# The expert chain of a decoder trunk set one pair further behind its gathers, its last phase written out

## The reference, cut to what matters

```python
s = jnp.einsum('nhie,ike->nhik', q, keys)          # 8 heads x 2 x 128 key scores per token
top_s, top_i = lax.top_k(s, 16)
...                                                # 16x16 candidates, the best 16 of them
idx  = jnp.take_along_axis(cand_i, best_pos, axis=-1)
gate = jax.nn.softmax(best_s, axis=-1)
u    = expert_u[idx]                               # 128 experts per token, each a row of 1024
act  = jax.nn.gelu(jnp.einsum('nhkd,nd->nhk', u, xb), approximate=False)
coef = gate * act
out  = jnp.einsum('nhk,nhkd->nd', coef, expert_v[idx])
h = h + out
```

## Time and profile before

| | before |
|---|---|
| median of three executions | 1802.99 us |
| the profiled execution: span | 1814.9 us |
| TensorE busy | 1521.3 us (84%) |
| VectorE busy | 1176.7 us (65%) |
| POOL busy | 597.8 us (33%) |
| ScalarE busy | 526.2 us (29%) |
| moved by DMA | 666.65 MB, mean 367 GB/s |

### The profile page before, as it was taken

The page is one execution under the profiler, slowest core; times in us unless marked ns, Lnnn a source line. Parts: engine busy times, 40 slices in busy tenths (PEclk is TensorE's granted clock), DMA queues, the critical chain, the costliest instruction groups (busy, mean ns, idle before and its releaser), DMA issues.

```text
span 1814.9 us, 18537 instructions
## 1 busy us (share of the span) xinstructions
PE 1521.3 (84%) x5336; PEld 826.6 (46%) x5336; DVE 1176.7 (65%) x3357; ACT 526.2 (29%) x1139; POOL 597.8 (33%) x588
## 2 busy tenths in 40 slices
PE   6858799897867899898988669989989888877776
PEld 3535343443544577454445436765544444432222
DVE  2478756655878666666458885666763778955554
ACT  0123212421233244353113323534521223321111
POOL 1032243443322322222332223333232334455442
PEclk9979799998988899999999889999989989999999
DMA  8399799999988799999998779999989989999997
GB/s 341 140 363 356 289 392 424 416 421 405 413 343 343 294 373 422 353 362 354 391 420 335 310 303 337 402 419 382 360 298 424 404 347 393 386 409 421 422 422 303
DMA packets 84050, 666.65 MB, mean 367 GB/s; under 512 B 9376, under 2 KB 9520, under 8 KB 10880
## 3 DMA queue, kind: packets, MB, share of 16 engines
q0 software_dynamic: 74464, 540.13, 74.9%
q1 hardware_dynamic: 9216, 124.47, 16.6%
q10 hardware_dynamic: 288, 1.05, 0.1%
HBM read 664.55 MB, written 1.05 MB: 367 GB/s over the span
## 4 chain that ended last, share of the span: by engine, by line
PE 52%; DVE 24%; DMA 12%; issue 5%; ACT 5%; POOL 1%; ACTq 0%; POOLq 0%; DVEq 0%; SPq 0%; PEldq 0%
PE acc L732 30%; DMA ring<-in_experts,idx_now 11%; PE act_bank L483 9%; DVE ring L1272 7%; PE dve_bank L469 6%; PE act_bank L669 3%; DVE scratch L939 3%; ACT diag L902 2%; DVE scratch L1182 1%; DVE scratch L1183 1%; DVE scratch L1185 1%; DVE scratch L1181 1%; ACT scratch L773 1%; DVE scratch L1184 1%; PE dve_bank L649 1%
## 5 line engine op out<-in xcount | busy, mean ns | idle before, releaser
L732 PE MATMUL acc<-ring,diag 128*128 128x512 f32 x2048 | 1007.5, 630 | 258.3 <-ACT diag L902 251.1
L411 POOL DMA_INDIRECT ring<-in_experts,idx_now x512 | 570.9, 1115 | 910.2 <-PE acc L732 815.5
L1272 DVE CUSTOM_DVE_ANT_0 ring<-ring,hn 128x1024 f32<-128x1024 f32 x512 | 623.4, 1224 | 252.3 <-DMA ring<-in_experts,idx_now 235.9
L732 PEld LDWEIGHTS acc<-ring,diag 128*128 128x128 f32 x2048 | 383.1, 198 | 724.9 <-issue 423.7
L895 ACT ACTIVATE acts<-dots 128x2 f32<-128x2 f32 x256 | 52.1, 204 | 766.8 <-DVE dots L1272 760.8
L483 PEld LDWEIGHTS act_bank<-hnT,wbuf 128*128 128x128 f32 x1920 | 245.8, 202 | 55.1 <-issue 55.1
L902 ACT ACTIVATE diag<-cst,coefs 128x128 f32<-128x128 f32 x512 | 177.9, 394 | 248.9 <-DVE coefs L1280 224.9
L483 PE MATMUL act_bank<-hnT,wbuf 128*128 128x128 f32 x1920 | 245.8, 284 | 1.2 <-ACT hnT L773 1.2
L773 ACT ACT_TABLE_LOAD x82 | 105.2, 1283 | 23.2 <-PE act_bank L669 14.4
L406 POOL COPY idx_now<-idx 128x8 uint32 x64 | 21.4, 334 | 260.8 <-PE acc L732 186.6
L1280 DVE TENSOR_TENSOR coefs<-acts,gate 128x2 f32<-128x2 f32 x256 | 41.2, 161 | 92.4 <-ACT acts L895 81.5
(11 more groups left out here) (112 smaller groups left out, 819.4 us busy)
## 6 DMA issues: line engine op xcount, KB each, us to landing
wbuf<-in_weights SPq DMA_DIRECT2D x56, 2048.0 KB
ring<-in_experts,idx_now POOLq DMA_INDIRECT x512
kept<-in_weights SPq DMA_DIRECT2D x2, 2048.0 KB, 14.6
gains<-in_gains SPq DMA_DIRECT2D x2, 512.0 KB, 8.5
scratch<-in_bias POOLq DMA_DIRECT2D x1, 1024.0 KB, 7.8
gains<-in_gains ACTq DMA_DIRECT2D x2, 512.0 KB, 10.3
out<-h SPq DMA_DIRECT2D x2, 512.0 KB, 8.8
scratch<-in_bands POOLq DMA_DIRECT2D x1, 768.0 KB, 4.5
```

Of the source, the lines that this page charges most:

```text
L411: pool.indirect_dma_start(ring[:, s], None, io[f"experts{layer}"], bass.IndirectOffsetOnAxis(idx_now[:, j * RING + s:j * RING + s + 1], 0) ...
L732: ins = pe.matmul(acc[half], diag[:, n % DIAGS], ring[:, slot, D + half * CW:D + (half + 1) * CW], start=start, stop=stop, skip_group_chec ...
L1272: dve.tensor_tensor_reduce(out=ring[:, slot, 0:D], in0=ring[:, slot, 0:D], in1=hn[:, phase % NBLK], scale=1.0, scalar=0.0, op0=ALU.mult, o ...
```

## The change

It adds `LAG = 2 * GROUP` (4 slots) and takes out `UNROLLED` and the loops of the last phase; all four phases are now written out on VectorE, ScalarE and TensorE. The order for slot `n` becomes:
- VectorE: `dot(n)`, side work, and after an odd slot `coefficients(p - 1)`; the last pair's follow at the phase's end;
- ScalarE: `take_gelu(p)`, side work, `make_diagonals(p - 1)`; the last pair's at the phase's end;
- TensorE: `sum_slot(n - 4)`, then side work.

The ring, the number of diagonal buffers, the pace, POOL's and SyncE's streams and all waits inside the helpers stay as they are.

```diff
-UNROLLED = {0: STEPS, 1: STEPS, 2: STEPS, 3: 4}
+LAG = 2 * GROUP
...
 # TensorE
             def experts(phase, beside):
                 first = phase * STEPS
-                looped = first + UNROLLED[phase]
-
-                total = UNROLLED[phase] * BODY
-                for n in range(total + GROUP):
-                    if n == GROUP and phase:
+                for n in range(SLOTS + LAG):
+                    if n == LAG and phase:
                         pe.wait_ge(sem("acc_read"), phase)
-                    if n >= GROUP:
-                        at = n - GROUP
+                    if n >= LAG:
+                        at = n - LAG
                         sum_slot(first + at // BODY, at % BODY, start=at == 0, stop=at == SLOTS - 1)
-                    if n < total:
+                    if n < SLOTS:
                         beside.upto(pace(phase, n))
-                if looped < first + STEPS:
-                    with pe.Fori(looped, first + STEPS - 1) as g:
-                        for n in range(BODY):
-                            sum_slot(g, n)
-                    for n in range(BODY):
-                        sum_slot(first + STEPS - 1, n, stop=n == BODY - 1)
 # ScalarE
             def experts(phase, beside):
-                first = phase * STEPS
-                looped = first + UNROLLED[phase]
-                for n in range(UNROLLED[phase] * BODY):
-                    g, q = first + n // BODY, n % BODY // GROUP
+                first = phase * STEPS * GROUPS
+                for n in range(SLOTS):
+                    at = first + n // GROUP
                     if n % GROUP == GROUP - 1:
-                        take_gelu(g, q)
+                        take_gelu(at // GROUPS, at % GROUPS)
                     beside.upto(pace(phase, n))
-                    if n % GROUP == GROUP - 1:
-                        make_diagonals(g, q)
-                if looped < first + STEPS:
-                    with act.Fori(looped, first + STEPS) as g:
-                        for q in range(GROUPS):
-                            take_gelu(g, q)
-                            make_diagonals(g, q)
+                    if n % GROUP == GROUP - 1 and n >= GROUP:
+                        make_diagonals((at - 1) // GROUPS, (at - 1) % GROUPS)
+                make_diagonals(at // GROUPS, at % GROUPS)
 # VectorE
             def experts(phase, beside):
-                first = phase * STEPS
-                looped = first + UNROLLED[phase]
-                for n in range(UNROLLED[phase] * BODY):
-                    g = first + n // BODY
-                    dot(phase, g, n % BODY)
+                first = phase * STEPS * GROUPS
+                for n in range(SLOTS):
+                    at = first + n // GROUP
+                    dot(phase, at // GROUPS, n % BODY)
                     beside.upto(pace(phase, n))
-                    if n % GROUP == GROUP - 1:
-                        coefficients(phase, g, n % BODY // GROUP)
-                if looped < first + STEPS:
-                    with dve.Fori(looped, first + STEPS) as g:
-                        for n in range(BODY):
-                            dot(phase, g, n)
-                            if n % GROUP == GROUP - 1:
-                                coefficients(phase, g, n // GROUP)
+                    if n % GROUP == GROUP - 1 and n >= GROUP:
+                        coefficients(phase, (at - 1) // GROUPS, (at - 1) % GROUPS)
+                coefficients(phase, at // GROUPS, at % GROUPS)
```

## The result

The changed kernel takes 1912.22 us (median of four runs, 1908.98 to 1933.72) against 1806.35 us (median of four too). The ratio, taken without the one execution of the kernel before that lasted 3936.03 us, is 1.063, with a 95% interval of 1.0568 to 1.0693. So the changed kernel is 6% slower; the forecast was 1821 us, with a range up to 1860. The span of its profiled execution is 1907.1 us against 1814.9: 92 us more.

What follows compares the result with a forecast made beforehand. Bound taken as a relay of engines and DMAs: TensorE busy 84%, DMA share 1.00 in four long stretches. Gelu -9, ring +16, phase ends +11, written-out code 0: +18 on 1803 gives 1821 us, range 1785 to 1860.

Steps and rivals of the forecast that it cites:

- the lag leaves the engines' alignment alone: TensorE's wait for diagonals and ScalarE's for `coefs` stay, each above 150 us; only gelu leaves this path.
- Part 3: Phase ends, two pairs left to sum: +3.4 us at the last, 2.5 at each other; sum +11, bounds +3 and +15.
- the last phase: Looped part of the last phase: ring trip 18.6 us less 0.3 against 19.8, 1.5 us to spare, so loss 0.
- part 1: Gelu off VectorE's path: gain only in the four routing stretches where VectorE sets the pace, -9 us; bounds 0 and -23.
- part 2: Ring holds each row two slots more: loss once per hand-over from engines to DMAs, +16 us; bounds 0 and about +45.
- 3.3 us are left: At 223 to 506 us: trip 19.8 us plus side work between dot and sum, against a limit of 23.1 us.
- the slower rival: Ring too short at 2.9 us a slot if side work exceeds the 3.3 us left: 47 us, 1850 us; chance 0.15.
- The prediction's own sign: Prediction is wrong if VectorE's wait for rows grows by more than 60 us outside the last phase.
- what POOL's wait was taken for: POOL waits for sums for 815.5 us in all, listed under how often DMAs stand still because the ring is full.

Runs made afterwards that it cites:

- the run with the loops back: Changed kernel with the lag only up to slot 64 of the last phase, the last 64 slots as the old loops without lag: 1905.76 us, ratio 1.0575.
- the fourth run: Kernel before with coefficients and diagonals of a pair ahead of the side work of its odd slot, TensorE's order untouched: 1805.12 us, ratio 0.9993.

## Why the prediction was wrong, point by point

**Right: the lag leaves the engines' alignment alone.** TensorE's wait for diagonals is 276.7 us and ScalarE's for `coefs` 176.7, both above the 150 named, and the gelu wait is gone.

**Part 3: the last end right, the others too small.** The changed kernel's last dot and what follows (timeline, as the earlier trace rows):

```profile
1893.26 1.22 DVE L1258 CUSTOM_DVE_ANT_0 ring<-ring,hn 128x1024 f32<-128x1024 f32 x1 [1.21 <-DMA ring<-in_experts,idx_now]
...
1895.37 7.13 PE L732 MATMUL acc<-ring,diag 128*128 128x512 f32 x16 [1.23 <-ACT diag L893]
1902.54 1.41 DVE L925 TENSOR_TENSOR h<-h,acc 128x512 f32<-128x512 f32 x2 [7.62 <-PE acc L732]
```

Two pairs are summed in 7.13 us, the wait before `h` is 7.62 instead of 4.60, where near 8 was forecast. From the last dot to the end it is 3 us more. The four waits of this kind together, before and after:

```profile
DVE h L939 <- PE acc L732: 19.6, 4, 5.4
```

```profile
DVE h L925 <- PE acc L732: 35.6, 4, 11.2
```

16 us more where the sum had 11. The inner ends were charged 2.5 us each. By the timelines they went from 4.57, 5.42 and 5.05 us to 7.93, 8.80 and 11.23: 3.4 us more at two of them and 6.2 at the third. Why the third took so much more stays open.

**Nearly right: the last phase.** The trip there was worked out to 1.5 us short of full, and most slots ran at 2.48 us. The chain's pieces there, slots 432 to 511, shrank from 12.54 us to 7.55 to 10.09, where 7.5 was foreseen:

```profile
1773.64 10.09 DMA ring<-in_experts,idx_now
...
1870.83 7.55 DMA ring<-in_experts,idx_now
1885.02 8.22 DMA ring<-in_experts,idx_now
```

But the 1.5 us were not there. The landing was taken from the first gather, 5.7 us. In slots 432 to 499 of the changed kernel an even slot's rows land after 8.1 us in the mean and after 6.6 at the least; its hold time is 12.0 and the release 0.9, where the prediction had 12.6 together. So even with the quickest landing the trip is 19.5 of 19.8 us, and in the mean it is 21.0. Stretches of the changed kernel, then one of before; the last three columns are granted clock, DMA share and GB/s:

```profile
1700.00:1770.00 70.00, 50.03 (x109) 19.37 (x108) 34.32 (x68) 11.02 (x42) 30.59 (x31) 1.00 1.00 408
1776.50:1780.00 3.50, 3.50 (x6) 1.45 (x5) 2.27 (x5) 0.00 (x0) 0.24 (x1) 0.52 1.02 433
1817.50:1821.00 3.50, 3.36 (x4) 1.52 (x5) 1.76 (x3) 0.08 (x1) 0.07 (x1) 0.51 1.00 421
1834.70:1838.00 3.30, 3.30 (x4) 1.34 (x5) 1.78 (x3) 0.00 (x0) 0.00 (x0) 0.50 1.00 425
```

```profile
1700.00:1770.00 70.00, 52.17 (x115) 20.18 (x113) 37.17 (x71) 12.56 (x42) 35.02 (x32) 1.00 1.01 422
```

Some microseconds ran at half clock, and sums took longer there: 16 matmuls 8.8 us, against 7.13 in the row above. But the first of these stretches had the whole clock and still moved 408 GB/s against 422, so the half clock isn't the only cause. With no queue in between, each delay reaches the DMAs. Slots 432 to 511 lost 8 us, and the run with the loops back gets them back.

**Wrong: part 1.** The 9 us for gelu were not seen: ten places with the lag are no faster than eight without, and the fourth run put 60 us more of this wait on VectorE without a change in time (it shortened the hold time too, so this is no clean test of the wait).

**Wrong, and the step that failed: part 2.** It said that what is lost is lost once at each hand-over from engines to DMAs, 5 us at three or four places, +16, at most +45. Measured: slots 32 to 511 lost 91 us, of which the three inner phase ends can explain some 13; the rest, near 78, I put down to the ring, and two more places take nearly all of the loss away.

The trip round the ring was computed in full for the looped part of the last phase alone, where there is no side work. For 223 to 506 us it stopped at "3.3 us are left" and never set a price against it, though this was the very condition of the slower rival. The numbers were there to be read. The hold time in that stretch was 9.3 us before, so after it would be 9.3 + 2 x 2.9 = 15.1 (measured 15.5). The landing wasn't that of the first gather, 5.7 us: it took 7.5 to 9.9 us in those slots of before whose rows lay ready 5 us and more (112 to 223 and 256 to 335; means over groups of 24 to 48 slots), and 9.2 here afterwards. Gathers are let go in twos there and share the DMA engines with weight chunks; but in slots 432 to 499 of the changed kernel, where no weights are loaded, it is 8.5 all the same. With 1.4 for the rest, 15.1 + 9.2 + 1.4 = 25.7 us a trip, 3.2 us a slot, against 3.23 measured.

That is 0.3 us for each of 96 slots, some 30 us of the 41 in this stretch, and more in others. Counted as the prediction did, for an even slot of 40 to 111: of the 3.3 us left, side work between dot and gather took 2.7 (15.8 + 1.0 measured, less 3 x 2.9 + 5.4), and the longer landing 3.2 (8.9 against 5.7). The sum put the second of these at nothing. The prediction's own sign for this came true: VectorE's wait for rows outside the last phase grew from 146.4 to 357.3 us, far more than the 60 that it named. A loss that recurs with every trip was booked as one that occurs at a crossing.

**The rival that came true** was the ring that becomes too short. It had the right mechanism and condition, a chance of 0.15, and a price of 47 us: a tenth of a slot time in 470 us. Slots 32 to 127 lost 14% and slots 384 to 431 13%, 59 us in these two alone. It was to be decided by a landing 1.5 to 3.3 us above the 5.7 of an empty queue, that is 7.2 to 9.0; the means were 7.5 to 9.9.

**Wrong: what POOL's wait was taken for.** I read the 815.5 us for which POOL waits for sums as a ring that is full and could give something up. The run with seven places, 1.4% slower, shows that the old order had less than one place to spare.

## What to carry to other kernels

A ring of n places gives at best n slots per trip: add issue, landing (as measured among other traffic), waiting, hold time and release, in every kind of stretch, and compare with n times the slot time. In this kernel, where the two were within a place of each other, a longer pipeline between fetch and release cost like a smaller ring, at every trip. Here the lag was harmless only together with more places, and the wait that it removed, from an engine that mostly didn't set the pace, paid for none of it.

## What the runs showed that I had not expected

The cost of a place is steeply bent: 8 us for want of each of the ninth and tenth, 27 us for the eighth, 99 us for the seventh. Order on one engine and data dependence are different things: TensorE's sums set two slots back cost 1.8%, and the same set back by a product that needs the next rows 6.3%. And TensorE's granted clock, 1.00 throughout slots 432 to 511 before (1606.5 to 1803.9 us), fell to 0.50, the lower of its two levels (1.2 GHz), three times in the same slots of the changed kernel. Two of the falls, about 1776.6 and 1834.7 us, came just as these sums had begun, which had waited longer than the usual 1.2 us (timeline):

```profile
1775.88 7.54 PE L732 MATMUL acc<-ring,diag 128*128 128x512 f32 x13 [3.05 <-ACT diag L893]
...
1834.58 6.68 PE L732 MATMUL acc<-ring,diag 128*128 128x512 f32 x11 [3.37 <-ACT diag L893]
```

So late rows may cost twice, by the wait and by the slower sums after it. But the length of one wait doesn't decide it: the third fall, about 1817.6 us, came with a wait of 2.15 us, while one of 2.95 us in the kernel before (1611.42) and one of 2.42 in the changed one (1754.05) passed at 1.00. What lets the clock fall was not tried by itself.
